# Moving 24 gathered value rows from the expert search into the key search, and the slots of three tiles three or four blocks later

## The chip, the core and the metric

The kernel runs on one core of one Trainium2 chip. The metric is the device time of one execution in microseconds; the median of three runs of the kernel before is 3742.21 us (3740.44 to 3743.11). PE is TensorE, DVE is VectorE, ACT is ScalarE, POOL is GpSimd, SP is SyncE.

## The reference, cut to what matters

Two layers over 128 prompt tokens (tile 0) and 512 latent tokens (tiles 1 to 4). Each layer is attention and gating, and then a retrieval of experts:

```
q = (x @ w_q) ... s1 = q0 . key1, s2 = q1 . key2        # 8 heads, 128 keys each side
t1, i1 = top_k(s1, 16); t2, i2 = top_k(s2, 16)          # "keys"
top, pos = top_k(t1 + t2, 16); idx = i1 * 128 + i2      # "choose": 128 experts of 16384 for each token
a = u_tab[idx] . x                                      # dots
w = gelu(a) * softmax(top)
out = sum(w * v_tab[idx])                               # adds
x = layer_norm(alpha * x + gate * out)
```

So each token needs 128 rows of `u_tab` (1024 floats each) dotted with it, and 128 rows of `v_tab` added up with weights.

## The kernel before, in words

**Two ways to the experts.** Tiles 3 and 4 go the dense way: PE multiplies them with all 16384 rows of `u_tab`, in 128 blocks of 128 experts (the u stage, L929), and with all of `v_tab`, in 128 blocks (the v stage, L957). Between the two lie gates: for every token of tiles 3, 4 and 1 a pair of one-hot matrices (DVE at L1449 and L1454, part of them by ACT) is multiplied on PE (L941) into a 128x128 map of its 128 weights, four tokens to a "chunk", 32 chunks to a tile. ACT copies each chunk out (L1172), and four chunks make a "part", of which ACT stores half in DRAM (L1179) and SP the other half (L540, `store_gates`). Tiles 0 and 2 go the gathered way: for each of 128 slots POOL gathers one row for each of 128 tokens with an indirect DMA (L668) into a ring of 8 buffers (`ring`, `GP = 8`), and DVE dots it with the tile (`dot_rows`, L1290, `prompt_rows` for tile 0) or adds it (`add_rows`, L1308; the first at L1311). Tile 1 has its u rows gathered and its v rows dense. One row is 128 x 4 KB, 0.524 MB.

**Order of the gathers.** POOL walks the list `ROWS`: 128 u rows of tile 0, v rows 0 to 63 of tile 0, 128 u rows of tile 1, then the rest. It is never more than 8 rows ahead of DVE, and before the first row of a tile it waits for that tile's expert numbers (`idx_ready`, written at L1401 at the end of `choose`).

**Order on DVE.** DVE's program is one list in a fixed order, and the rows are spread over it by hand. In the latent group (`g == "S"`): 28 prompt rows; 40 within attention; 8 more; the residual and norm of the four tiles (L1594 to L1604); 24 rows; then the 16 steps j of `first_tile_keys` (top 16 of each of tile 1's 16 key scores, L1316 to L1325), with 28 prompt rows in steps 0 to 7, the weights of tile 0 (`expert_weights(0)`) in step 10 and 40 v rows in steps 10 to 15; then the six steps of `choose` for tile 1. After that come 22 steps of `choosing(3, i)` with 24 v rows and 16 u rows of tile 1, `slots_out(3)`, 22 steps of tile 3's one-hots with `choosing(4, i)`, `slots_out(4)`, the rest of tile 3's one-hots, tile 4's one-hots with 78 u rows of tile 1, `slots_out(1)`, and tile 1's one-hots with 16 v rows of tile 0.

**Order on PE.** The queries and keys of the latent group (L903 in four rounds n of 27.5 us, L915 after each), then `u_order`: the 128 blocks of the u stage, with three jobs `slT` (L934, they turn a tile's slots and wait for its `slots_out`) after the blocks in `SLOT_BLOCKS`, and the chunks placed by `chunk_block`. Four PSUM banks hold u blocks, two hold chunks. The table of `u_tab` streams through `w_ring` on SP's queue, 8 blocks (4 MB) ahead.

**Order on ACT.** ACT follows the same `u_order` (L1139 for a block) and has four calls of `top_softmax` or `gelu_dots` in between, at fixed blocks. In the key search its step j takes query j out of PSUM (L1104) and then key j-1 (L1110, L1114); `gelu_dots(0)` stands at step 10 and waits for the last prompt dot.

**End of the u stage.** `gates_with(i)` puts the SP half of a part at the load i with `(b + 9) // 2 == i`, where b is the block of the part's last chunk; i = 64 is load 0 of the v stage. At load 1 of the v stage SP waits for block 123, loads, waits until every part is stored, and only then loads the first gates (L563) and activations (L559), which DVE (L1464) needs for the first v block:

```
for i in range(KEYS // 2):                    # the v stage, SP
    ... wait for block 120 + 2 * i + 1 (while b < WR), load peer_vB
    for part in gates_with(KEYS // 2 + i):
        store_gates(part)
    if i == 1:
        for j in range(3):
            sp.wait_ge(gate_out[j], (l + 1) * 32 * PLACED[j])
        load_gates(0)
```

Of the kernel before, what the change touches and what calls it, by code (L numbers as in the profile page):

```python
# [32 lines left out]
SLOTS = PH * TOPK  # L33
# [9 lines left out]
GP = 8  # L43
# [42 lines left out]

SLOT_BLOCKS = {50: 3, 78: 4, 103: 1}

SEARCH_CHUNKS = 22


def chunk_block(k, q):

    if k == 3:
        return 52 + q if q < SEARCH_CHUNKS else 73 + (q - SEARCH_CHUNKS) // 2
    first, blocks = {4: (80, 23), 1: (105, 16)}[k]
    return first + blocks * q // CHUNKS


# [173 lines left out]
def build(nc, x_prompt, x_sample, cache_k, cache_v, cond, w_mod, b_mod, w_in, sg_ln_g, sg_ln_b,  # L275
# [10 lines left out]
    with ExitStack() as ctx:  # L286
# [76 lines left out]
        first = left[:].rearrange("p (h j) -> p h j", h=PH)  # L363
# [602 lines left out]
        def _(act):  # L966
# [3 lines left out]
            for l in range(DEPTH):  # L970
# [96 lines left out]
                for gi, (g, tiles) in enumerate(GROUPS.items()):  # L1067
                    nt = len(tiles)
                    modulation("begin")
                    if g == "P":  # L1070

                        act.wait_ge(emptied[BANK["modT", 3 * l]], emptied_at(("modT", 3 * l), 0))
                    for c in range(DC):
                        job = ("xT", g, c)
                        act.activation(hT[:, c, 0:nt * P], ready(job)[:, 0:nt * P], ACT.Identity,  # L1075
                                       scale=mcol[:, l, 8 + c, gi:gi + 1],
                                       bias=mcol[:, l, c, gi:gi + 1]).then_inc(emptied[BANK[job]], 1)
                    if g == "P" and l:
                        act.wait_ge(cond_in, 16 * (l + 1))
                        act.activation(cT, cT, ACT.Silu).then_inc(silu_done, 1)  # L1080
                    if g == "S":
                        top_softmax(0)
                    projected(g, 2, su)
                    if g == "S":
                        job = ("cT", g)
                        act.activation(kT[:, 4, :], ready(job)[:, 0:P], ACT.Copy).then_inc(emptied[BANK[job]], 1)
                    job = ("kT", g)
                    act.activation(kT[:, 0:nt, :].rearrange("p t n -> p (t n)"), ready(job)[:, 0:nt * P], ACT.Copy
                                   ).then_inc(emptied[BANK[job]], 1)
                    attend(g)  # L1090
                    modulation("attended")
                    for t in range(nt):
                        for half in range(2):
                            job = ("hT", g, t, half)
                            act.activation(hT[:, 4 * half:4 * half + 4, t * P:(t + 1) * P],
                                           ready(job)[:, :].rearrange("p (c n) -> p c n", c=4), ACT.Copy
                                           ).then_inc(emptied[BANK[job]], 1)
                    for j in range(2 * PH + 1):
                        if g == "S" and j == 10:
                            gelu_dots(0)  # L1100
                        if j < 2 * PH:

                            job = ("query", g, j)
                            act.activation(qh[:, j % 2, 0:nt * P], ready(job)[:, 0:nt * P], ACT.Copy  # L1104
                                           ).then_inc(emptied[BANK[job]], 1)
                        if j:
                            job = ("keys", g, j - 1)
                            src = ready(job)
                            if g == "S":
                                act.activation(scores[:, :, j - 1, :], src[:, P:4 * P].rearrange("p (t n) -> p t n", n=P),  # L1110
                                               ACT.Copy)
                                if j > 8:
                                    act.wait_ge(key_used, l * (2 * PH) + (j - 8))
                            act.activation(key_ring[:, (j - 1) % 8, :] if g == "S" else prompt_keys[:, j - 1, :], src[:, 0:P],  # L1114
                                           ACT.Copy).then_inc(emptied[BANK[job]], 1)
                            if j == 4:
                                modulation("turned")
# [15 lines left out]
                for job in u_order():  # L1133
                    if job[0] == "u":
                        b = job[1]
                        if b % 2 == 0 and b // 2 >= ACT_BUFS:
# [1 line left out]
                                        16 * (l * (BATCHES // ACT_BUFS) + b // 2 // ACT_BUFS))  # L1138
                        act.activation(act_st[b // 2 % ACT_BUFS][:, b % 2, :], ready(job)[:, 0:TOKENS], ACT.Gelu_apprx_tanh  # L1139
                                       ).then_inc(emptied[BANK[job]], 1)  # L1140
                        if b == 18:
                            top_softmax(1)
                        if b == 43:
                            top_softmax(3)
                        if b == 68:
                            top_softmax(4)
                        if b == 102:
                            gelu_dots(1)
                    elif job[0] == "slT":
                        k = job[1]  # L1150
# [14 lines left out]
                    else:  # L1165
                        _, k, q = job
# [28 lines left out]
        def _(dve):  # L1195
# [8 lines left out]
            for l in range(DEPTH):  # L1204
# [80 lines left out]
                def dot_rows(k, lo, hi):  # L1285

                    for row in range(lo, hi):
                        b, uses = row_at(l, "u", k, row)
                        dve.wait_ge(row_full[b], (uses + 1) * 16)
                        dve.scalar_tensor_tensor(ring[:, b, :], ring[:, b, :], 1.0, h2[:, k, :], ALU.mult, ALU.mult,  # L1290
                                                 accum_out=dots[:, k, row:row + 1]).then_inc(row_used[b], 1)
# [3 lines left out]
                def prompt_rows(n):  # L1295

                    dot_rows(0, prompt_row[0], prompt_row[0] + n)
                    prompt_row[0] += n
# [298 lines left out]
                def norm_modulate(g, t):  # L1597

                    k = GROUPS[g][t]
                    layer_norm_stats(x[:, k, :], D)  # L1600
                    link(scaled(x[:, k, :], x[:, k, :], mv[:, 0:1], rstd[:, 0:1], row5[g][LN1G], row5[g][LN1B]))
                    dve.wait_ge(late_rows_in, (2 * l + (list(GROUPS).index(g) + 1)) * 32)
                    link(dve.tensor_tensor(h2[:, k, :], x[:, k, :], row5[g][SCALE2], ALU.mult))
                    dve.tensor_tensor(h2[:, k, :], h2[:, k, :], row5[g][SHIFT2], ALU.add).then_inc(h2_ready, 1)  # L1604
                    dve.wait_ge(h2_ready, l * TILES + (k + 1))

                for gi, (g, tiles) in enumerate(GROUPS.items()):
                    nt = len(tiles)
                    latent = g == "S"
                    modulation("begin")  # L1610
                    for n in range(2):
                        for t in range(nt):
                            take_qk(g, n, t)
                    if l and not latent:

                        for t in range(1, len(V_DENSE)):
                            close_tile(t, l - 1)
                    if latent:
                        prompt_rows(28)
                    modulation("projected")  # L1620
                    dve.wait_ge(layer_in, (l + 1) * (16 * 8))
                    attend(g)
                    modulation("attended")
                    if latent:

                        prompt_rows(GP)
                    dve.wait_ge(rows_in, (2 * l + (gi + 1)) * 48)
                    for t in range(nt):
                        for n in range(2):
                            residual(g, n, t)  # L1630
                        norm_modulate(g, t)
                    if latent:
                        prompt_rows(SLOTS - 28 - 40 - GP - 28)
                    modulation("summed")
                    for j in range(2 * PH):
                        if latent and j < 8:
                            prompt_rows(3 + j % 2)
                        if latent and j == 10:
                            expert_weights(0)
                        if latent and j >= 10:  # L1640
                            add_rows(0, 40 * (j - 10) // 6, 40 * (j - 9) // 6)
                        first_tile_keys(g, j)
                    for step in range(6):
                        choose(tiles[0], step)

                for i in range(2 * PH + 6):
                    if i < 12:
                        add_rows(0, 40 + 2 * i, 42 + 2 * i)
                    else:
                        dot_rows(1, 16 * (i - 12) // 10, 16 * (i - 11) // 10)  # L1650
                    choosing(3, i)
                slots_out(3)
                for i in range(2 * PH + 6):
# [97 lines left out]
```

## Time and profile before

| | |
|---|---|
| median of three runs | 3742.21 us |
| the profiled execution, device time | 3742.21 us |
| its span in the profile | 3740.4 us |
| mean granted clock of TensorE | 0.958 of full speed |
| PE busy | 3462.9 us, 93% |
| DVE busy | 2776.1 us, 74% |
| POOL busy | 1618.5 us, 43% |
| DMA | 1263.48 MB, mean 338 GB/s |

Times within a view count from the start of the span. The first layer's latent key search runs from 476 to 607 us, its u stage from 607 to 1194 us and its v stage from 1195 us to about 1860 us; the second layer repeats them from 2313, 2444 and 3032 us. "[9.55 <-X]" at the end of a row says that the engine was idle for 9.55 us before it and that X ended the wait.

### The profile page before, as it was taken

The numbers are of one execution on the slowest core, as the hardware profiler recorded it, in microseconds if no ns is written. First come the engines' busy times: TensorE is split into PE (matmuls) and PEld (weight loads), VectorE is DVE, ScalarE is ACT, GpSimd is POOL, SyncE is SP. The second block draws the span as 40 slices with busy tenths as digits, with TensorE's granted clock in tenths as the row PEclk, the third lists the DMA queues.
The fourth block names the chain that finished last, engine by engine and source line by source line (L and its number), as shares of the span: only waits on it lengthen the run. The fifth ranks groups of instructions, "written<-read, shape, count | busy, mean of one in ns | idle before, by whom it ended". The sixth has DMA issues, their size and how long they took to land.

```text
span 3740.4 us, 38317 instructions
## 1 busy us (share of the span) xinstructions
PE 3462.9 (93%) x12478; PEld 2110.3 (56%) x12478; DVE 2776.1 (74%) x6049; ACT 861.9 (23%) x2206; POOL 1618.5 (43%) x1362
## 2 busy tenths in 40 slices
PE   6898999999889999999988988999997999999997
PEld 2555446889777444444435554488886864444443
DVE  1488787999786876666756887789987867766668
ACT  1115211148632000000021260111675210000000
POOL 2034275423642354556510552644256323555553
PEclk9898999999899999999989989999998999999998
DMA  9866588989999899999974865899899998999995
GB/s 359 322 224 231 183 323 338 360 294 326 409 406 367 316 380 413 413 413 412 394 299 154 309 204 192 322 349 387 275 369 409 396 377 309 389 414 413 413 408 239
DMA packets 413989, 1263.48 MB, mean 338 GB/s; under 512 B 36240, under 2 KB 139664, under 8 KB 370784
## 3 DMA queue, kind: packets, MB, share of 16 engines
q0 software_dynamic: 192000, 721.61, 50.1%
q1 hardware_dynamic: 171808, 514.19, 36.6%
q10 hardware_dynamic: 49984, 25.23, 2.2%
q8 instruction: 101, 1.65, 0.2%
q14 instruction: 96, 0.79, 0.1%
HBM read 1174.06 MB, written 86.84 MB: 337 GB/s over the span
## 4 chain that ended last, share of the span: by engine, by line
PE 48%; DMA 23%; DVE 16%; issue 5%; POOL 5%; ACT 1%; SPq 1%; ACTq 0%; DVEq 0%; POOLq 0%
PE P L929 13%; DMA ring<-in_peer_v_dram,eidx 11%; DMA ring<-in_peer_u_dram,eidx 9%; PE P L903 7%; PE P L957 5%; POOL ring L668 5%; PE T L941 4%; PE P L737 4%; PE P L754 4%; DVE late L1308 3%; DVE ring L1290 2%; DMA ring<-in_w_mod_dram 2%; PE O L801 2%; PE T L737 2%; DMA acts_d<-late 1%
## 5 line engine op out<-in xcount | busy, mean ns | idle before, releaser
L668 POOL DMA_INDIRECT ring<-in_peer_u_dram,eidx x768 | 957.5, 1247 | 1142.7 <-DVE ring L1290 746.7
L1290 DVE SCALAR_TENSOR_TENSOR ring<-ring,h 128x1024 f32<-128x1024 f32 x768 | 925.3, 1223 | 277.9 <-DMA ring<-in_peer_u_dram,eidx 269.8
L957 PE MATMUL P<-w_ring,area 128*128 128x512 f32 x2048 | 931.2, 598 | 34.2 <-DVE area L1464 32.7
L668 POOL DMA_INDIRECT ring<-in_peer_v_dram,eidx x512 | 621.2, 1213 | 736.7 <-DVE late L1308 442.8
L929 PE MATMUL P<-hT,w_ring 128*128 128x256 f32 x4096 | 925.4, 385 | 0.5 <-DMA w_ring<-in_peer_uT_dram 0.5
L929 PEld LDWEIGHTS P<-hT,w_ring 128*128 128x128 f32 x4096 | 782.2, 194 | 104.3 <-issue 0.7
L957 PEld LDWEIGHTS P<-w_ring,area 128*128 128x128 f32 x2048 | 390.1, 192 | 537.9 <-issue 537.8
L1308 DVE SCALAR_TENSOR_TENSOR h<-ring,dots,h 128x1024 f32<-128x1024 f32 x254 | 325.8, 1283 | 155.1 <-DMA ring<-in_peer_v_dram,eidx 145.9
L1308 DVE SCALAR_TENSOR_TENSOR late<-ring,dots,late 128x1024 f32<-128x1024 f32 x254 | 325.6, 1282 | 22.1 <-DMA ring<-in_peer_v_dram,eidx 8.4
L903 PE MATMUL P<-hT,w_ring 128*128 128x128 f32 (+1 forms) x1024 | 287.8, 443 | 2.9 <-issue 2.9
L957 PE MATMUL V<-w_ring,qT 128*128 128x512 f32 x512 | 261.5, 592 | 0.0
L957 PE MATMUL O<-w_ring,qT 128*128 128x512 f32 x512 | 261.4, 592 | 0.0
L903 PEld LDWEIGHTS P<-hT,w_ring 128*128 128x128 f32 x1024 | 159.6, 197 | 127.4 <-issue 122.9
L1186 ACT ACTIVATE qT<-hT 128x128 f32<-128x128 f32 x128 | 39.6, 309 | 629.1 <-PE V L957 629.1
L1186 ACT ACTIVATE qT<-area 128x128 f32<-128x128 f32 x128 | 38.6, 308 | 592.5 <-PE V L957 592.5
L957 PEld LDWEIGHTS O<-w_ring,qT 128*128 128x128 f32 x512 | 97.3, 190 | 122.4 <-issue 122.4
L957 PEld LDWEIGHTS V<-w_ring,qT 128*128 128x128 f32 x512 | 97.3, 190 | 122.4 <-issue 122.4
L941 PE MATMUL T<-row 128*128 128x128 f32 x912 | 126.5, 287 | 38.7 <-issue 37.8
L941 PEld LDWEIGHTS T<-row 128*128 128x128 f32 x912 | 120.3, 200 | 49.1 <-issue 44.2
L737 PE MATMUL P<-w_ring,hT 128*128 128x512 f32 x320 | 144.9, 613 | 3.0 <-ACT hT L1075 3.0
L754 PE MATMUL P<-w_ring,hT 128*128 128x512 f32 x320 | 139.1, 593 | 1.5 <-issue 1.5
L1139 ACT ACTIVATE late<-P 128x256 f32<-128x256 f32 x128 | 48.5, 381 | 267.0 <-PE P L929 238.1
(227 smaller groups left out, 3276.3 us busy)
## 6 DMA issues: line engine op xcount, KB each, us to landing
w_ring<-in_peer_uT_dram SPq DMA_DIRECT2D x128, 1024.0 KB, 8.1
w_ring<-in_peer_vB_dram SPq DMA_DIRECT2D x128, 1024.0 KB, 8.0
ring<-in_w_mod_dram POOLq DMA_DIRECT2D x48, 1024.0 KB, 8.2
w_ring<-in_peer_wq_dram SPq DMA_DIRECT2D x64, 512.0 KB, 5.9
h<-acts_d SPq DMA_DIRECT2D x64, 512.0 KB, 8.8
w_ring<-in_w_in_dram SPq DMA_DIRECT2D x48, 512.0 KB, 4.9
area<-gate_d SPq DMA_DIRECT2D x16, 1536.0 KB, 14.4
hT<-gate_d SPq DMA_DIRECT2D x16, 1536.0 KB, 12.6
```

The lines of the kernel that those rows point to most:

```text
L668: pool.indirect_dma_start(out=ring[:, b, :], out_offset=None, in_=tables["uv".index(phase)], in_offset=bass.IndirectOffsetOnAxis(ap=eidx[: ...
L737: mm = pe.matmul(out[:, 0:width], hT[:, c, t * P:(t + 1) * P], w[:, c % 2, 0:width], start=c == 0, stop=c == DC - 1)
L754: mm = pe.matmul(out[:, :], hT[:, c, t * P:(t + 1) * P], w_ring[:, ws[4 * n + q], c % 2, :], start=c == 0, stop=c == DC - 1)
L801: mm = pe.matmul(out[:, :], v_pad[:, kb, HD * kv:HD * kv + P], pT[:, kv, i, :], start=kv == 0 and i == 0, stop=kv == 1 and i == len(keyb) - 1)
L903: mm = pe.matmul(out[:, 0:nt * P], w[:, c % 2, j * P:(j + 1) * P], hT[:, c, 0:nt * P], start=c == 0, stop=c == DC - 1)
L929: mm = pe.matmul(out[:, 0:TOKENS], w[:, c * P:(c + 1) * P], hT[:, c, TOKENS:2 * TOKENS], start=c == 0, stop=c == DC - 1)
L941: mm = pe.matmul(out[:, j * P:(j + 1) * P], oh_b[n % OH_BUFS][:, j, :], oh_a[n % OH_BUFS][:, j, :], start=True, stop=True)
L957: mm = pe.matmul(bank[ACC[2 * t + half]][:, :], w, uv_ring[:, b // 2 % (WR // 2), b % 2, half * 512:(half + 1) * 512], start=b == 0, stop= ...
L1139: act.activation(act_st[b // 2 % ACT_BUFS][:, b % 2, :], ready(job)[:, 0:TOKENS], ACT.Gelu_apprx_tanh).then_inc(emptied[BANK[job]], 1)
L1186: act.activation(wdot_T[:, b % 4, :].rearrange("p (s t) -> p s t", t=SUB), gate_in[b // 8 % 2][:, ACT_SUBS:SUBS, b % 8, :], ACT.Copy).then ...
L1290: dve.scalar_tensor_tensor(ring[:, b, :], ring[:, b, :], 1.0, h2[:, k, :], ALU.mult, ALU.mult, accum_out=dots[:, k, row:row + 1]).then_inc ...
L1308: dve.scalar_tensor_tensor(acc[k], ring[:, b, :], dots[:, k, row:row + 1], acc[k], ALU.mult, ALU.add).then_inc(row_used[b], 1)
```

## The change: what it does

No row of work is added or removed; only places in the fixed orders change. Of tile 0's 128 u rows, 15 instead of 8 stand after attention, 2 after each of the first three norms, and 39 instead of 24 after the last norm, so that none is left in the key steps 0 to 7. `gelu_dots(0)`, `expert_weights(0)` and the first v row move from step 10 to step 8, and steps 8 to 15 take 8 v rows each, 64 in all instead of 40. The 22 steps of `choosing(3, i)` keep only the 16 u rows of tile 1, spread evenly. In `u_order` the slots of tiles 3, 4 and 1 come after blocks 53, 81 and 107 instead of 50, 78 and 103; tile 3's chunks stand 3 blocks later, tile 4's start at block 83 instead of 80 and take 24 blocks instead of 23, tile 1's start at block 109 instead of 105 and take 14 blocks instead of 16. ACT's four calls follow.

```diff
-SLOT_BLOCKS = {50: 3, 78: 4, 103: 1}
+SLOT_BLOCKS = {53: 3, 81: 4, 107: 1}
...
     if k == 3:
-        return 52 + q if q < SEARCH_CHUNKS else 73 + (q - SEARCH_CHUNKS) // 2
-    first, blocks = {4: (80, 23), 1: (105, 16)}[k]
+        return 55 + q if q < SEARCH_CHUNKS else 76 + (q - SEARCH_CHUNKS) // 2
+    first, blocks = {4: (83, 24), 1: (109, 14)}[k]
     return first + blocks * q // CHUNKS
...
-                        if g == "S" and j == 10:
+                        if g == "S" and j == 8:
                             gelu_dots(0)
...
-                        if b == 18:
+                        if b == 28:
                             top_softmax(1)
-                        if b == 43:
+                        if b == 48:
                             top_softmax(3)
-                        if b == 68:
+                        if b == 72:
                             top_softmax(4)
-                        if b == 102:
+                        if b == 105:
                             gelu_dots(1)
...
-                        prompt_rows(GP)
+                        prompt_rows(15)
                     dve.wait_ge(rows_in, (2 * l + (gi + 1)) * 48)
                     for t in range(nt):
                         for n in range(2):
                             residual(g, n, t)
                         norm_modulate(g, t)
+                        if latent and t + 1 < nt:
+                            prompt_rows(2)
                     if latent:
-                        prompt_rows(SLOTS - 28 - 40 - GP - 28)
+                        prompt_rows(SLOTS - 28 - 40 - 15 - 6)
                     modulation("summed")
                     for j in range(2 * PH):
-                        if latent and j < 8:
-                            prompt_rows(3 + j % 2)
-                        if latent and j == 10:
+                        if latent and j == 8:
                             expert_weights(0)
-                        if latent and j >= 10:
-                            add_rows(0, 40 * (j - 10) // 6, 40 * (j - 9) // 6)
+                        if latent and j >= 8:
+                            add_rows(0, 8 * (j - 8), 8 * (j - 7))
                         first_tile_keys(g, j)
...
                 for i in range(2 * PH + 6):
-                    if i < 12:
-                        add_rows(0, 40 + 2 * i, 42 + 2 * i)
-                    else:
-                        dot_rows(1, 16 * (i - 12) // 10, 16 * (i - 11) // 10)
+                    dot_rows(1, 16 * i // 22, 16 * (i + 1) // 22)
                     choosing(3, i)
```

## Rows read from the trace of the kernel before

**Rows 1.** The page: the chain that ended last, shares of the span by engine.
```profile
PE 48%; DMA 23%; DVE 16%; issue 5%; POOL 5%; ACT 1%; SPq 1%; ACTq 0%; DVEq 0%; POOLq 0%
```

**Rows 2.** Waits of PE, 600 to 1200 us: total, times, longest.
```profile
PE T L941 <- issue: 28.9, 16, 3.3
PE O L934 <- DVEq L1436: 8.9, 1, 8.9
...
PE T L941 <- ACT area L1172: 0.6, 1, 0.6
```

**Rows 3.** Timeline of PE, u stage of the first layer: start, us, what.
```profile
792.41 0.66 PE L934 MATMUL O<-ident,r 128*128 128x128 f32 x2 [8.89 <-DVEq L1436]
...
793.08 9.30 PE L929 MATMUL P<-hT,w_ring 128*128 128x256 f32 x32
...
1195.01 3.67 PE L957 MATMUL P<-w_ring,area 128*128 128x512 f32 x8 [0.73 <-issue]
```

**Rows 4.** Groups of PE, 607 to 783.6 us: 16 records to a block.
```profile
L929 PE MATMUL P<-hT,w_ring 128*128 128x256 f32 x816 | 176.3, 379 | 0.0
```

**Rows 5.** Timeline of DVE around the norms and key steps, first layer.
```profile
416.15 0.69 DVE L1594 TENSOR_TENSOR tmp<-P,area 128x512 f32<-128x512 f32 x1 [9.55 <-DMA area<-in_ln_b_dram]
...
433.88 0.69 DVE L1594 TENSOR_TENSOR tmp<-P,area 128x512 f32<-128x512 f32 x1 [2.03 <-PE P L754]
...
473.38 1.22 DVE L1290 SCALAR_TENSOR_TENSOR ring<-ring,h 128x1024 f32<-128x1024 f32 x1
...
515.72 0.29 DVE L1316 MAX8 best<-key_ring 128x8 f32<-128x128 f32 x1
...
565.60 0.29 DVE L1316 MAX8 best<-key_ring 128x8 f32<-128x128 f32 x1 [8.11 <-ACT key_ring L1114]
```

**Rows 6.** Groups of DVE: 473.3 to 515.9, then 680.7 to 792.2 us.
```profile
L1290 DVE SCALAR_TENSOR_TENSOR ring<-ring,h 128x1024 f32<-128x1024 f32 x27 | 32.3, 1223 | 10.0 <-DMA ring<-in_peer_u_dram,eidx 9.8
...
L1308 DVE SCALAR_TENSOR_TENSOR late<-ring,dots,late 128x1024 f32<-128x1024 f32 x24 | 30.8, 1284 | 1.8
```

**Rows 7.** DVE's timeline; the ring in 560 to 660 us: who waited for it, landing.
```profile
648.62 0.29 DVE L1342 TENSOR_TENSOR probs<-best 128x128 f32<-128x128 f32 x1
...
680.70 2.68 DVE L1308 SCALAR_TENSOR_TENSOR late<-ring,dots,late 128x1024 f32<-128x1024 f32 x2
...
  DVE late L1308: 4.1, 4
...
DMA to landing us min/median/max: 5.4/8.5/17.6
```

**Rows 8.** DMA queues in 568 to 607, 607 to 650 and 650 to 735 us: packets, MB.
```profile
q0 software_dynamic: 1872, 6.82, 48.0%
...
q0 software_dynamic: 3062, 11.18, 65.9%
q1 hardware_dynamic: 1234, 6.20, 35.3%
...
q1 hardware_dynamic: 3541, 15.88, 49.6%
q0 software_dynamic: 3902, 14.21, 41.7%
```

**Rows 9.** Windows of all engines: span, busy times, PEclk, DMA share, GB/s.
```profile
568.00:607.00 39.00, 36.51 (x130) 19.94 (x129) 29.49 (x54) 8.98 (x22) 19.43 (x16) 1.00 0.71 255
...
923.00:1080.00 157.00, 128.72 (x649) 112.22 (x648) 121.88 (x221) 95.05 (x248) 105.58 (x82) 0.91 1.04 408
```

**Rows 10.** SP's queue and DVE at the end of the first u stage.
```profile
1174.50 0.38 SPq L540 DMA_DIRECT2D gate_d<-area  x1
1180.50 0.33 SPq L571 DMA_DIRECT2D w_ring<-in_peer_vB_dram  x1
...
1181.75 0.32 SPq L563 DMA_DIRECT2D area<-gate_d  x1
...
1191.40 0.42 DVE L1464 TENSOR_TENSOR area<-h,area 128x256 f32<-128x256 f32 x1 [29.72 <-DMA h<-acts_d]
```

## The prediction

> **What bounds the kernel now.** I read the page first. PE stands on 48% of the chain that ended last, DMA on 23% and DVE on 16% [rows 1]; no engine bounds the whole, so each stage has to be read by what its end waits for. The change touches only the stretch from the end of latent attention to the start of the v stage, in each of the two layers, so I read PE's waits of that stretch next. They are two: 8.9 us once, for DVE to hand out tile 3's slots after block 50, and 28.9 us in 16 waits for one-hots [rows 2]. The timeline puts the first at 792.41 us [rows 3]. Nearly all of the others fall between 923 and 1080 us, and there the window view shows the DMA engines full at 408 GB/s [rows 9]: DVE's one-hots stand in line behind dots whose rows have not landed. So from the slots of tile 3 to the slots of tile 1 DVE and the gathers lead and PE follows; after tile 1's slots PE leads again, until v starts at 1195.01 [rows 3].
>
> This gives the rule for the sum. If DVE reaches tile 3's slots s later than before, everything up to tile 1's slots moves by s, but PE then has four blocks fewer left to do (107 done instead of 103). A block costs 176.3 us / 51 = 3.46 us [rows 4], four cost 13.8 us. The v stage costs the same wherever it begins: its rows hang on its own blocks.
>
> **The change part by part.** *Prompt rows before the key search.* 13 more of them go where DVE is idle. Rows 9 to 15 after attention cost 7 x 1.15 us (one dot's start to the next) = 8.0 us in a gap of 9.55 us that ends with a DMA [rows 5]. POOL has to land them while DVE works, so the gap may be overrun by 2 us; the next residual waits 2.6 us for PE anyway, which covers it. Two rows after a norm cost 2.3 us against gaps of 2.03 us and twice 2.9 us [rows 5]; the 0.3 us too much goes into the next gap. Cost to PE 0. DVE work taken out of the later list: 14.9 us.
>
> *Rows before step 0.* DVE took 27 rows from 473.38 to 515.72, 32.3 us of work and 10.0 us idle, 9.8 us of it waiting for landings [rows 5, 6]. Now it takes 39. The 12 more come at the pace of the gathers, 1.6 us (the 42.3 us over 27 rows), so the last dot ends near 535 us. Key steps 0 to 6 then cost 7 x 1.83 = 12.8 us and end near 548. But step 7's key comes from ACT only at 565.60 [rows 5]: the idle time before it grows from 8.1 to 18 us. Most of what the gaps gave is lost here. `gelu_dots(0)` at ACT's step 8 now runs in ACT's idle time near 542 us; before, it made PE wait 1.6 us near 571. This gain of 1.6 us only lengthens PE's wait for tile 3's slots, so it counts 0.
>
> *The v rows, where I expect the cost.* From 567.4 us DVE needs 1.2 us for the weights and then, eight times, 8 adds of 1.38 and a key step: 12.9 us. With every row there it would end step 15 at 671.8. By 607.3 it has used 24 rows; 8 more are asked for, of which those asked in the last 6 us are still on the way (least time to landing 5.4 us [rows 7]): 28 landed. From 607 us on the stream of the u stage shares the DMA. Between 607 and 650 the gather queue landed 11.18 MB, 21.3 rows, while both queues moved 404 GB/s; over 650 to 735 the other queue took 15.88 MB, 187 GB/s [rows 8]. So 49.3 rows are there at 650, and the other 14.7 come at 0.524 MB / (404 - 187 GB/s) = 2.4 us each: the last near 685 us, 15 us after DVE could have used it. With 1.3 us for the add and 1.8 us for the key step DVE ends step 15 at 688.1 instead of 648.62 [rows 7]. Before, the DMA was used for only 255 GB/s in 568 to 607 [rows 9], because DVE had nothing to ask; this is still so for half of that time.
>
> *Choosing.* The six steps for tile 1 take 680.70 - 648.62 = 32.1 us [rows 7], to 720.2. Then a new wait: after row 63 POOL may not gather until tile 1's numbers are out, so the ring is empty, where before 24 v rows stood between and the u rows came behind them unseen. The first row is asked at about 720.5, lands 5.4 us later at the earliest [rows 7], and DVE wants it after one key step of 1.8 us: 4 us. Then `choosing(3)`: 111.5 us before, less 24 adds at 1.30 us net (30.8 us busy [rows 6]), 80.3 us. Slots at 804.5 instead of 792.2: s = 12.3 us. PE was at the old place at 783.5; three blocks later, less the 1.6 us, it is at the new one at 792.3, and waits 12 us instead of 8.9.
>
> A rule of the Trainium skill bears on the 2.4 us: DMA: Bandwidth & Descriptors, section Queues, rings and completion order, says that each of the 16 engines goes round the queues with work, a packet at a time. If that gave each of the two queues half of the 404 GB/s, a row would take 2.6 us, the last would land 3 us later, and the kernel would take 3761 us. The row of 650 to 735 has the stream below a half, so I keep 2.4.
>
> *To tile 1's slots.* One block more is loaded and stored in the full stretch, 0.524 + 0.131 MB at 408 GB/s [rows 9]: +1.6 us.
>
> *The squeezed chunks.* Tile 1's 32 chunks lie in 14 blocks instead of 16, 2.4 us a chunk on PE; DVE was ahead of PE there and stays so. The stores of the parts get 1.7 us less each before their buffer is wanted again, and PE already waited 0.6 us for one [rows 2]; at that chunk it now stands one block (3.5 us) earlier. Bounds 0 and 3.5; I take 1.5, since that wait came once.
>
> *The end of the stage.* Tile 1's last chunk moves from block 120 to 122 while the stage still ends with 127. (120 + 9) // 2 = 64 and (122 + 9) // 2 = 65: the last part's store on SP slips from load 0 of the v stage, after block 121, to load 1, after block 123, right in front of the wait for all stores. Before: issued 1174.50, landed 7.2 us later, and the gates were asked for at 1181.75, 1.25 us after block 123; DVE started 9.65 us later [rows 10]. Now the store is issued 0.9 us after block 123 and lands 8.1 us after it, gates asked, DVE starts 17.8 us after block 123, PE 0.6 later, 18.4, where PE itself is free after 13.8 and before started after 14.5: +3.9 us. Nothing else hides this: DVE and ACT wait for the same loads. A PE idle that long may also bring the clock down to 1.2 GHz: after the 8.89 us, two blocks took 9.30 us instead of 6.9 [rows 3, 4]. Bounds 0 and 2.2, I take 1.1.
>
> ACT's calls cost nothing where they are put: exp for tile 1 is ready near 701 and asked for at block 28 (707), and the others likewise lie behind DVE's new times. At the old block 18 (673 us) it would have held ACT for 28 us.
>
> **Sum for a layer:** 12.3 + 1.6 - 13.8 + 1.5 + 3.9 + 1.1 = +6.6 us. The second layer repeats the first stage by stage, so 13 us in all on 3742.2 us, which is both the profiled execution and the median: 3755 us.
>
> **Rivals.** *The gathers keep up.* Then step 15 ends at 671.8, slots are out near 788, PE finds them at block 53, s = 0: 1.6 - 13.8 + 1.5 + 3.9 + 1.1 = -5.7 us a layer, 3731 us. For it: before, DVE waited only 4.1 us for v rows up to 647, in four waits [rows 7]. Against it: all four came at the end of that stretch, and the 36 rows wanted after 607 are 18.9 MB, at the wanted pace 325 GB/s beside 187. It decides at s = 5.7: if the last v row lands before 679, the change is a gain.
>
> *The end of the stage is hidden*, because the store lands sooner than 7.2 us or ACT and PE start on less. Then +1.6 us a layer, 3745 us. Against it: SP waits for all three store semaphores in a fixed order.
>
> *The rows crowd out PE's stream* between 607 and 690. The stream may run dry for some blocks, but PE has 12 us to give before block 53; rows come faster, so this leads to the first rival or to none.
>
> **How the numbers follow.** A slower kernel by the sum, 3749 to 3776: 0.5. Gathers keep up or nearly: 0.22, of it most below 3734. End hidden, or s some 4 us less by a landing at 681: 0.28, 3735 to 3749. The bounds of one layer are landing 680 to 690 (-5, +5), first row 2 to 5 us (-2, +1), pressure 0 to 3.5, clock 0 to 2.2; all low ends give -2.9, all high ends +15.7, so -6 to +31 in all. The range takes in the first rival: 3731 to 3773. Measured against 0.2%, 7.5 us, about what this kernel's runs can tell: faster 0.22, same 0.28, slower 0.50. Of the likeliest alone: 3749 to 3773.
>
> **What would show it.** Right: PE's wait at L934 near 12 us, after block 53; waits of DVE for `in_peer_v_dram` rows of 12 us or more between 607 and 690; one wait of some 4 us for the first u row of tile 1; a wait of 4 to 5 us of PE at the first v block, released by DVE or ACT behind `gate_d`; v starts 6 us later. Wrong: no wait at L934 (gathers kept up), or v's first block right behind block 127. What would break the sum is a DMA split other than in the rows before, since s enters one to one and twice.

## The result, and the profile after

The change makes the kernel slower: 3779.76 us (median of four runs) against 3741.47 us, a ratio of 1.0104 with a 95% interval of 1.0087 to 1.0121. That is 38 us where the sum said 13, and above the top of the range, 3773 us. The profiled execution of the changed kernel took 3784.16 us, so the terms read from its trace add up to 42 us and not to 38.

PE's waits in the same stretch of the first layer (total, times, longest) are to be compared with [rows 2]:

```profile
PE T L941 <- issue: 26.9, 16, 5.0
PE O L934 <- DVEq L1436: 16.8, 1, 16.8
PE P L957 <- DVE area L1464: 4.1, 1, 4.1
PE T L941 <- ACT area L1172: 3.4, 1, 3.4
```

The wait for tile 3's slots did not go away. It nearly doubled (8.9 us before), and the first v block has a wait of its own. PE's timeline, to be compared with [rows 3]:

```profile
816.10 0.66 PE L934 MATMUL O<-ident,r 128*128 128x128 f32 x2 [16.78 <-DVEq L1436]
...
1216.85 6.10 PE L957 MATMUL P<-w_ring,area 128*128 128x512 f32 x8 [4.06 <-DVE area L1464]
```

Tile 3's slots are 23.7 us later than before (792.41), and v starts 21.8 us later (1195.01 before). In the second layer v starts at 3071.05 instead of 3031.59, which adds another 17.6 us. DVE's timeline, to be compared with [rows 5], shows where that began:

```profile
411.77 1.23 DVE L1290 SCALAR_TENSOR_TENSOR ring<-ring,h 128x1024 f32<-128x1024 f32 x1 [3.14 <-DMA ring<-in_peer_u_dram,eidx]
415.74 1.23 DVE L1290 SCALAR_TENSOR_TENSOR ring<-ring,h 128x1024 f32<-128x1024 f32 x1 [2.73 <-DMA ring<-in_peer_u_dram,eidx]
...
425.95 0.69 DVE L1594 TENSOR_TENSOR tmp<-P,area 128x512 f32<-128x512 f32 x1
...
572.72 0.29 DVE L1316 MAX8 best<-key_ring 128x8 f32<-128x128 f32 x1 [19.16 <-ACT key_ring L1114]
```

The seven extra rows after attention had not landed when DVE wanted them. It waited five times, 9.9 us in all, and the first residual stands at 425.95 instead of 416.15. The next lines are the last v row, the start of `choose` for tile 1 and the first row of tile 1, to be compared with [rows 7]:

```profile
695.12 1.28 DVE L1308 SCALAR_TENSOR_TENSOR late<-ring,dots,late 128x1024 f32<-128x1024 f32 x1 [1.65 <-DMA ring<-in_peer_v_dram,eidx]
698.16 0.29 DVE L1342 TENSOR_TENSOR probs<-best 128x128 f32<-128x128 f32 x1
...
737.58 1.22 DVE L1290 SCALAR_TENSOR_TENSOR ring<-ring,h 128x1024 f32<-128x1024 f32 x1 [5.51 <-DMA ring<-in_peer_u_dram,eidx]
```

The group view of DVE from 574.5 to 698.2 us sums the waits up (busy, mean ns, idle before it and what ended it), and the DMA view of 613 to 696 us, the stretch in which the rows shared the DMA with the u stage's stream, shows why:

```profile
L1308 DVE SCALAR_TENSOR_TENSOR late<-ring,dots,late 128x1024 f32<-128x1024 f32 x63 | 80.9, 1284 | 26.9 <-DMA ring<-in_peer_v_dram,eidx 22.8 <-DVE best_ix L1325 0.4
```

```profile
DMA packets 8326, 33.86 MB, mean 408 GB/s; under 512 B 935, under 2 KB 935, under 8 KB 6824
...
q0 software_dynamic: 5205, 18.92, 56.5%
q1 hardware_dynamic: 3116, 14.87, 44.0%
```

The DMA is full. The gathers got 18.92 MB, 36.1 rows in 83 us or 2.3 us a row on average; DVE wanted one in 1.6. The average hides two parts. From 613 to 650 us the gathers got 9.57 MB, 259 GB/s. From 650 to 696 us the split was even:

```profile
q0 software_dynamic: 2575, 9.35, 50.2%
q1 hardware_dynamic: 2003, 9.16, 49.1%
```

That is 203 GB/s for the gathers, 2.6 us a row, and 199 GB/s for the stream and its stores.

### The profile page after: what moved, and what is told of

The parts are those of the page before. It is cut to its first block, busy times and chain, and to the rows that moved or that the text cites. A ratio compares the mean times of both kernels' runs of the same rounds, so it can differ in the third digit from the quotient of the medians.

```text
span 3782.3 us, 38327 instructions
## 1 busy us (share of the span) xinstructions
PE 3467.4 (92%) x12478; PEld 2111.3 (56%) x12478; DVE 2781.4 (74%) x6049; ACT 861.9 (23%) x2206; POOL 1578.6 (42%) x1362
## 4 chain that ended last, share of the span: by engine, by line
PE 42%; DMA 27%; DVE 17%; issue 5%; POOL 5%; SPq 2%; ACT 1%; ACTq 0%; DVEq 0%; POOLq 0%
DMA ring<-in_peer_v_dram,eidx 12%; PE P L929 11%; DMA ring<-in_peer_u_dram,eidx 10%; PE P L903 6%; PE P L957 6%; POOL ring L668 5%; PE T L941 4%; PE P L737 4%; DVE ring L1290 2%; DVE late L1308 2%; DMA ring<-in_w_mod_dram 2%; SPq L550 2%; PE T L737 2%; PE V L957 1%; PE O L957 1%
## 5 line engine op out<-in xcount | busy, mean ns | idle before, releaser
L668 POOL DMA_INDIRECT ring<-in_peer_u_dram,eidx x768 | 932.4, 1214 | 1259.1 <-DVE ring L1290 778.9
L668 POOL DMA_INDIRECT ring<-in_peer_v_dram,eidx x512 | 606.4, 1184 | 703.9 <-DVE late L1308 377.0
L754 PE MATMUL P<-w_ring,hT 128*128 128x512 f32 x320 | 139.1, 593 | 1.5 <-issue 1.5
L737 PEld LDWEIGHTS P<-w_ring,hT 128*128 128x128 f32 x320 | 63.2, 199 | 83.3 <-issue 79.3
```

The lines of the kernel that those rows point to most:

```text
L668: pool.indirect_dma_start(out=ring[:, b, :], out_offset=None, in_=tables["uv".index(phase)], in_offset=bass.IndirectOffsetOnAxis(ap=eidx[: ...
L737: mm = pe.matmul(out[:, 0:width], hT[:, c, t * P:(t + 1) * P], w[:, c % 2, 0:width], start=c == 0, stop=c == DC - 1)
L754: mm = pe.matmul(out[:, :], hT[:, c, t * P:(t + 1) * P], w_ring[:, ws[4 * n + q], c % 2, :], start=c == 0, stop=c == DC - 1)
```

## The experiments

Each timed run is a ratio to the kernel before on the same chip in the same hours (medians of the kernel before: 3741 to 3745 us). Absolute times in two traces are not comparable to the last microsecond. PE's last projection of attention (L754), before which no edit changes anything, starts at 406.14 us before, 407.05 in the changed kernel, and between 402.8 and 409.4 us in the others. Where "counted from L754" is said, this is taken out.

**Eight rows after attention.**

```diff
-                        prompt_rows(15)
+                        prompt_rows(8)
...
-                        prompt_rows(SLOTS - 28 - 40 - 15 - 6)
+                        prompt_rows(SLOTS - 28 - 40 - 8 - 6)
```

> The changed kernel with one number back: 8 prompt rows after attention instead of 15, the other 7 before key step 0 (46 instead of 39). Theory (the 15 rows cost PE directly): the trace of the changed kernel has DVE's first residual at 425.95 us instead of 416.15 and key 7 at 572.72 instead of 565.60. With 8 rows the residual is back near 416, key 7 near 565.6, the 46 dots end near 545 and keys 0 to 6 near 558, still before key 7. So 7 us a layer come back: about 3766 us, a ratio to the kernel before of 1.006 to 1.007. Rival (the delay at the norms is swallowed later and the v rows alone cost the time): no change, 3776 to 3783 us.

Measured: 3770.89 us, ratio 1.0066 (1.0044 to 1.0088), as expected. The interval just overlaps that of the changed kernel (1.0087 to 1.0121), but the trace is clear. The first residual starts at 413.09, released by a DMA as in the kernel before, and PE gets to the slots 6 us earlier counted from L754, still with a wait of 16.8 us. So the late front (the seven extra rows, which hold up the norms and everything behind them) is worth about 0.4%, and most of the loss is elsewhere.

**V rows spread again.** From the changed kernel, 5 v rows a key step and the other 24 in `choosing(3)`:

```diff
-                            add_rows(0, 8 * (j - 8), 8 * (j - 7))
+                            add_rows(0, 5 * (j - 8), 5 * (j - 7))
...
-                    dot_rows(1, 16 * i // 22, 16 * (i + 1) // 22)
+                    if i < 12:
+                        add_rows(0, 40 + 2 * i, 42 + 2 * i)
+                    else:
+                        dot_rows(1, 16 * (i - 12) // 10, 16 * (i - 11) // 10)
```

> The changed kernel with the v rows as before: 40 within the key steps (5 in each of steps 8 to 15), 24 within choosing(3), and the 16 u rows in its last ten steps. All else as changed. Theory (64 rows want more DMA than the stream leaves, and DVE stands for them before the numbers of tile 1): step 15 ends near 650 us instead of 698, slots of tile 3 out near 794, PE reaches them at block 53 without a wait near 800: 16 us a layer come back, about 3747 us, ratio 1.000 to 1.003. Rival (the gathers cost the same time wherever they stand, since the bytes are the same): slots as late as in the changed kernel, 3775 to 3783 us.

Measured: 3745.05 us, ratio 1.000 (0.999 to 1.001), as expected. Step 15 of the key search ends at 644.15 instead of 698.16, and PE takes tile 3's slots without a wait:

```profile
644.15 0.29 DVE L1342 TENSOR_TENSOR probs<-best 128x128 f32<-128x128 f32 x1
...
798.27 0.38 PE L934 MATMUL O<-ident,r 128*128 128x128 f32 x2
```

This one edit gives back everything that the change cost, although the first residual is nearly as late as in the changed kernel (426.04; 7.4 us later than before counted from L754, where the changed kernel has 8.9).

**V rows packed alone**, on the kernel before (8 per step, weights and gelu at step 8, 16 u rows alone in `choosing(3)`, two ACT calls moved):

```diff
...
-                        if latent and j == 10:
+                        if latent and j == 8:
                             expert_weights(0)
-                        if latent and j >= 10:
-                            add_rows(0, 40 * (j - 10) // 6, 40 * (j - 9) // 6)
+                        if latent and j >= 8:
+                            add_rows(0, 8 * (j - 8), 8 * (j - 7))
...
```

> The kernel before with only the v rows moved: weights of tile 0 and ACT's gelu at step 8, 8 v rows in each of steps 8 to 15, 16 u rows alone in choosing(3), ACT's two calls at blocks 28 and 48. Prompt rows and blocks as before. Theory (by the steps on record: last v row near 685 us, step 15 done at 688, an empty ring for 4 to 5.5 us, slots at 804 instead of 792): PE waits 21 us at L934 instead of 9, and all after it moves with it: 12 us a layer, 3765 to 3770 us, ratio 1.005 to 1.008. Rival (without the late front the rows land in time): ratio 0.998 to 1.001.

Measured: 3777.42 us, ratio 1.0083 (1.0064 to 1.0102), a little more than foreseen. PE takes the slots 16.7 us later than before, counted from L754; the prediction had 12.3. PE's waits:

```profile
PE O L934 <- DVEq L1436: 27.1, 1, 27.1
PE T L941 <- issue: 23.4, 13, 3.7
```

**Half the stream.** The changed kernel, with the first 24 blocks of the u stage loading half of their bytes. It leaves out half of each of these table rows, so it does not compute the right activations for them; it only serves to show the timing:

```diff
+                    part = slice(0, D // 2) if i < 12 else slice(0, D)
-                    sp.dma_start(uv_ring[:, i % (WR // 2)], peer_uT[l, i])...
+                    sp.dma_start(uv_ring[:, i % (WR // 2), :, part], peer_uT[l, i, :, :, part])...
```

> The changed kernel, but the first 24 blocks of the u stage load only half of their bytes (the halves of each row of the table that are left out keep what the ring held, so the activations of those 24 blocks are not computed from the right data). PE's work and all semaphores stay. Theory (the v rows wait because the stream shares the DMA): while DVE wants them, 607 to 696 us, the stream asks for 75 GB/s less, a row takes 1.8 us instead of 2.3, DVE's idle time for v rows falls from 19 us to 5 or less, and step 15 ends 14 us or more earlier than 698. Rival (POOL's issue or the ring's depth sets the pace of the rows): idle time and step 15 unchanged within 3 us.

There is one run, 3739.25 us, and only its trace of the first layer is used. DVE's waits from 560 to 740 us, first of the changed kernel, then of this one (its line numbers are two higher):

```profile
DVE late L1308 <- DMA ring<-in_peer_v_dram,eidx: 22.8, 22, 2.0
DVE best L1316 <- ACT key_ring L1114: 19.2, 1, 19.2
DVE ring L1290 <- DMA ring<-in_peer_u_dram,eidx: 5.5, 1, 5.5
```

```profile
DVE best L1318 <- ACT key_ring L1116: 18.6, 1, 18.6
DVE ring L1292 <- DMA ring<-in_peer_u_dram,eidx: 5.0, 2, 3.1
DVE late L1310 <- DMA ring<-in_peer_v_dram,eidx: 5.0, 9, 0.8
```

The rows, POOL's program, the ring of 8 and PE's work are the same, and only the stream is smaller. The wait for v rows falls from 22.8 to 5.0 us, and step 15 ends 18.5 us earlier (679.7 instead of 698.2; 16.8 us counted from key 7). So neither POOL's issue nor the depth of the ring alone sets the pace here: what the stream takes from the DMA does.

**Prompt rows alone**, on the kernel before (15, then three times 2, then 39, none in the key steps).

> The kernel before with only the prompt rows' places changed (15 after attention, 2 after three norms, 39 before step 0, none in steps 0 to 7); the weights of tile 0 stay at step 10, 40 v rows after them, blocks as before. Theory: the 15 rows overrun the gap by 10 us, of which PE loses 6 to 7 us a layer before the u stage, and DVE's key 7 comes 7 us later; tile 3's slots move as much as PE does, so the wait at L934 stays near 9 us: +13 us, 3755 to 3760 us, ratio 1.003 to 1.004. Rival (the overrun costs only beside concentrated v rows): ratio 0.999 to 1.001.

Measured: 3751.77 us, ratio 1.0027 (1.0016 to 1.0038), a little less than foreseen. DVE waits five times, 8.8 us in all, for rows in front of the first residual. Key 7 finds DVE 18 us idle, and the wait at L934 is 9.4 us, much as before.

**Block places alone**, on the kernel before, with the chunks and ACT's four calls moved along.

```diff
-SLOT_BLOCKS = {50: 3, 78: 4, 103: 1}
+SLOT_BLOCKS = {53: 3, 81: 4, 107: 1}
...
-    first, blocks = {4: (80, 23), 1: (105, 16)}[k]
+    first, blocks = {4: (83, 24), 1: (109, 14)}[k]
```

> The kernel before with only the places in the block order changed (slots after blocks 53, 81, 107, the chunks and ACT's four calls with them); rows on DVE as before. By the terms on record: no wait for tile 3's slots (+1.5), +1.6, -13.8, +1.5, +3.9, +1.1 = -4.2 us a layer, 3733 us. By the sizes that the trace of the changed kernel shows from tile 3's slots on (+4.2 to tile 1's slots, then -6.1 to v, +2.4 of slow clock), 1.5 + 4.2 - 6.1 + 2.4 = +2 us a layer, 3745 us. Both have the wait at L934 gone and a wait of 3 to 5 us at the first v block. Rival (the blocks themselves are the loss): slower by 10 us or more.

Measured: 3743.36 us, ratio 0.9995 (0.9986 to 1.0005): no change. The wait of 8.9 us at L934 is gone and came back in three places: 34.9 us instead of 28.9 for one-hots, 2.2 instead of 0.6 for ACT's copy, 4.5 instead of 0.7 at the first v block.

The three parts alone give +0.83, +0.27 and -0.05%, together 1.05% against 1.04% measured. That the sum comes out so well is in part luck. The run with v rows spread has about the last two together and measures 0.00% instead of 0.22, a difference just clear of the intervals. The likely reason, argued and not tested by itself, is that the later blocks pay for a late front.

**Last store early.** From the changed kernel:

```diff
-    return [part for part, b in enumerate(ends) if (b + 9) // 2 == i]
+    return [part for part, b in enumerate(ends) if min((b + 9) // 2, KEYS // 2) == i]
```

> The changed kernel with the last part's store on SP back at load 0 of the v stage (the load index is capped at 64), so that it is issued once block 122's chunks are out of PSUM and not behind block 123. Theory (the start of v hangs on this store): it is issued some 3 us earlier, the first v block starts 3 us earlier, PE's wait there falls from 4.1 to about 1 us and the slow clock behind it (6.1 us for the first 8 matmuls instead of 3.7) goes: 5 us a layer, about 3769 us. Rival (the gates' and activations' own loads set the start): wait and time unchanged, 3776 to 3783 us.

Measured: 3774.69 us, ratio 1.0083 (1.0062 to 1.0103), against 1.0104 of the changed kernel; 3769 us was foreseen. The intervals overlap, so the time by itself does not show a gain. The timeline shows the start of v repaired:

```profile
1209.85 3.67 PE L957 MATMUL P<-w_ring,area 128*128 128x512 f32 x8 [0.73 <-DVE area L1464]
```

The wait is 0.73 us instead of 4.06, and the first eight matmuls take 3.67 us again instead of 6.10.

**Better versions.** The three repairs on the changed kernel at once (v rows spread, eight rows after attention, last store early):

> The changed kernel with the three repairs at once: v rows spread (as in the run with 40 and 24), 8 prompt rows after attention, the last store at load 0. If the terms add: 1.000 less 6.5 us a layer for the front and less 4 us a layer for the start of v: 3722 to 3728 us, ratio 0.994 to 0.996. If they are not independent (the front's gain turns into a wait elsewhere): 0.998 or more.

Measured: 3727.41 us, ratio 0.9957 (0.9947 to 0.9968), as expected. Next, this order of the rows with the block places of the kernel before:

> The kernel before with its own block places and ACT calls, but 8 prompt rows after attention, 2 after three norms, 46 before step 0, weights of tile 0 at step 8, 5 v rows in each of steps 8 to 15, 24 in choosing(3). Theory (DVE's time to tile 3's slots leads until tile 1's slots): slots are out near 783 us, PE is at block 50 near 782, the wait of 8.9 us and its slow clock go, and all up to tile 1's slots moves 9 us earlier: 3722 to 3727 us, ratio 0.994 to 0.996. Rival (only PE's blocks count): PE's wait moves into the one-hots, ratio 0.999.

Measured: 3723.32 us, ratio 0.9945 (0.9924 to 0.9967), as expected. PE takes tile 3's slots after block 50 with a wait of 1.6 us. Last, v rows from step 7 on, with the blocks placed for it (slots after blocks 48 and 76):

```diff
...
+                        if latent and j < 6:
+                            prompt_rows(3)
+                        if latent and j == 7:
                             expert_weights(0)
+                            add_rows(0, 0, 10)
+                        if latent and j >= 8:
+                            add_rows(0, 10 + 5 * (j - 8), 10 + 5 * (j - 7))
...
```

> As the run with the new rows and the old blocks, and further: 28 prompt rows before step 0 and 3 in each of steps 0 to 5, the weights of tile 0 and 10 v rows in step 7, where DVE waits for key 7, then 5 v rows a step (50 by step 15), 14 in choosing(3). Slots of tile 3 after block 48, of tile 4 after 76, tile 4's chunks in 25 blocks from 78. Theory (the cost of v rows depends on when the DMA is free: 255 GB/s between 568 and 607 us before): 10 rows cost DVE nothing, slots come near 773 us, all up to tile 1's slots moves 17 us earlier less 3 us for two more blocks in the full stretch: 14 us a layer, 3710 to 3718 us, ratio 0.991 to 0.994. Rival (the early rows only bring forward the same DMA limit): no better than the run without them, 0.995 or more.

Measured: 3718.76 us, ratio 0.9932 (0.9912 to 0.9952), as expected. It has the lowest median and is faster than both kernels, but its interval overlaps that of the run before it, so the last step is not shown to be a gain. DVE starts tile 0's weights at 547.79 instead of waiting for key 7. It takes the last v row of step 15 before 633, waits 0.2 us for v rows between 560 and 700 us, and PE takes tile 3's slots at 771.49. The stream now has to give: PE waits 5.4 us for blocks of the u table.

## Why the prediction was wrong in its size, by its own steps

The way was right, and so was the mechanism of the largest term, the v rows. But one term was put at zero and most others were too small. Per layer the sum put the start of v 5.5 us later (6.6 less 1.1 of slow clock behind it); the first layer shows 21.8. Of the missing 16 us the late front is 7.1, the v rows 2.9, the empty ring 1.5, the full stretch 2.6 and the end of the stage 2.3. (These are differences between two single traces; 0.9 us of the first is already there at L754.)

- *Rows 9 to 15 after attention, "Cost to PE 0".* This is the step that failed outright. I let POOL overrun the gap by 2 us and said that the next wait for PE would cover it. The first residual was 9.8 us late and key 7 was 7.1 us late (8.9 and 6.2 counted from L754), and the u stage started 4.5 us later, counted the same way. The prediction never asked how long a row takes to land in this stretch. The waits for rows end at 411.77, 415.74, 418.30, 422.07 and 423.52, one in 2.9 us. Five broadcasts of norm rows, 0.5 MB each, were loaded in the same stretch, and a gathered row took 11.3 us from issue to landing (median). The run with eight rows gives back 0.4%, and the prompt rows alone cost 0.27%, so this step explains 10 to 14 of the 25 us that the sum is short. Whether POOL's issue (one in 2.3 us up to 409 us) or the broadcasts made it so was not separated.
- *The v rows.* This was right in kind: the DMA is full and DVE stands for the rows. The 28 rows that I had landed when the u stage begins fit too (36.1 landed after that, 64 in all). The size was too small: DVE ended step 15 19.2 us after it could have (key 7 at 572.72, the 106.2 us from key 7 to the end that the prediction gives with every row there, end at 698.16), where I had 16.3. The pace up to 650 was as foreseen, 259 GB/s for the gathers. Behind 650 the gathers had 203 GB/s and not 217, so a row took 2.6 us and not 2.4, which is 3 us over the last 15 rows. My 187 GB/s for the stream came from 650 to 735 us of the kernel before, where both queues together moved only 355 GB/s. That row showed what the stream asks for, not how a full DMA is shared.
- By the Trainium skill, DMA: Bandwidth & Descriptors, section Queues, rings and completion order, each engine goes round its queues a packet at a time. The prediction priced an even split at 2.6 us a row and set it aside. The trace agrees with the even split in 650 to 696 us: 9.35 against 9.16 MB and 2.6 us a row. That taking turns is the cause is not shown: by my own estimate the stream asks for 0.655 MB in every block of 3.46 us, 189 GB/s, which is not far from the 199 that it got.
- *The empty ring.* The wait was 5.5 us instead of 4. With the front and the v rows this makes s = 12.3 + 7.1 + 2.9 + 1.5 = 23.8 us; measured 23.7.
- *The full stretch* from tile 3's to tile 1's slots was 4.2 us longer in the changed kernel and 2.5 in the run with blocks alone, where I had 1.6 for one more block. The rest stays open.
- *The end of the stage.* From tile 1's slots to v it took 107.8 us instead of 113.9 in the kernel before, so -6.1 where the sum had -8.4. PE's wait for the stored parts rose by 2.8 us (from 0.6 to 3.4), near the upper bound and not 1.5. The slipped store cost less than foreseen: a wait of 4.06 us instead of 0.73, so 3.3 us against 3.9. The slow clock behind it cost 2.4 us in the first layer and 1.7 in the second, against 1.1. The run with the store early shows the wait and the slow clock gone. The remaining 1.6 us of this stretch stay open.
- *The blocks.* By the terms of the sum the later blocks alone were worth 4.2 us a layer, 3733 us. They measured 3743.36, no gain: they remove the wait of 8.9 us, but PE then stands for DVE's one-hots and at the end instead. That later blocks pay for a delay of DVE seems right: with the v rows spread and the blocks late, a front that alone costs 0.27% costs nothing that can be measured.
- The rival "the gathers keep up" is out by the packed run and the half stream: only with half the stream do they nearly keep up. The top of the range left no room for an error in the front, which enters twice, once in each layer.

## What to carry to other kernels

A gap of an engine is only free for work whose data is there. Before moving transfers into a gap, read what else is on the DMA in it, and take the time to landing of that stretch, not the best one. How two queues share a full DMA can only be read from a stretch in which it is full. Where transfers compete with a stream that may not wait, put them where the DMA has room (here 10 rows one step earlier, where it moved 255 GB/s before). Packed together they make the engine that waits for them stand, and the prefetch ring that is empty behind them costs one more time to landing. And in a kernel with a fixed order, moving a consumer later on the engine that follows hides a wait but does not shorten the list of the engine that leads.

## What the runs showed of the hardware

With both queues at work, 650 to 696 us of the changed kernel, the gathers moved 9.35 MB and the stream with its stores 9.16 MB, 403 GB/s in all. Taking 4.7 MB from the stream (14.87 to 10.15 MB in 613 to 696 us) took 18 us of waiting from DVE. A gathered row of 0.5 MB took 16.2 us from issue to landing there (median), 10.5 with half the stream, and 5.4 at the least in the kernel before.

After a wait of 4.06 us PE's first eight matmuls took 6.10 us instead of 3.67. The granted clock was 0.50 from 1216.8 to 1220 us, the lower of its two levels. After 0.73 us of waiting they took 3.67. The length of the wait alone does not decide it: in the second layer 2.83 us of waiting were followed by 5.37 us in the changed kernel, and 3.63 us by 3.67 us, at a granted clock of 1.00, in the run with v rows spread.
